# Starting a decoder-layer kernel with three matrix products of its cross-attention memory

## The chip, the cores and the metric

The kernel runs on one core of one Trainium2 chip. The time is device microseconds of one execution. Three runs of the kernel before took 683.46, 684.13 and 684.65 us (median 684.13). The profiled execution took 683.86 us, of which 682.0 us lie between its first and its last instruction.

## What is computed

One layer of a hybrid decoder over 256 tokens of width 1024, in float32. The normed input goes through one wide projection whose columns feed three branches: causal attention with 8 heads, a state-space scan with 4 groups, and cross-attention into 256 memory tokens with 4 heads. Gates merge the three, then come an output projection, a convolutional feed-forward network and a last norm. Cut to what the change touches:

```python
u = rms_norm(x, mix_norm_g)
proj = u @ w_in                      # q, k, v, z, xBC, dt, memory queries qm, three gates
kv = rms_norm(mem, mem_norm_g) @ w_mem_kv
km, vm = split(kv)                   # 4 heads of 256 columns each
s = (qm / 16) @ km.T                 # per head
o_mem = softmax(s) @ vm
merged = g0 * (o_attn @ w_br_attn) + g1 * (o_ssm @ w_br_ssm) + g2 * (o_mem @ w_br_mem)
h = x + merged @ w_out
out = rms_norm(h + conv_glu(rms_norm(h, ffn_norm_g)), final_norm_g)
```

A norm's factor is one number per memory token, so `rms_norm(mem) @ w` equals `factor * ((mem * mem_norm_g) @ w)`: the factor may be applied to the product.

## The kernel before, in words

**Chunks.** Every weight matrix passes through in chunks of 1 MB. Three slots (`w_raw`, 8 KB of each partition apiece) take them in turn, so a chunk is known by its round `r` and its slot `s`. For each chunk SyncE issues two DMAs (`load`, L292, or `load_wide`, L311) as soon as the slot's previous chunk has been split; ScalarE rounds it to `w_hi` (`split_hi`, L328) once TensorE is done with the slot's previous chunk; VectorE subtracts to get `w_lo` (`split_lo`, L334); and TensorE multiplies three times for each pair of operands, hi by hi, hi by lo and lo by hi (`three`, L362). A chunk of 256 columns is the moving or stationary side of 48 matmuls with 256 columns (`gemm_cols`, L339); a "wide" one, 512 rows by 512 columns, is the moving side of 24 matmuls with 512 columns (`wide_part`, L368).

**Order.** Nothing is scheduled by a compiler. Each engine's instructions stand in the order in which the source writes them, each engine runs its own queue strictly in that order, and semaphores hold it. So an instruction that waits holds up everything behind it on its engine.

**Start.** SyncE loads `x` first (L459, L460), then small tables and the first chunk of `w_in`. TensorE issues 13 matmuls on zeros meanwhile (`keep_warm`, L409, called at L585), then a small product for the attention bias, then turns `x` with 16 transposes (L600), after ScalarE's squares (L951), GpSimd's power (L1795) and VectorE's scaling (L1292). `tok_hi` (L963) and `tok_lo` (L1306) are split from the turned `x` column block by column block, and the first product, `first_part` (L604), follows.

**Stages.** Four groups of the scan (rounds 0 to 7), attention (`heads`, rounds RB = 8 to 11), memory and gate 1 (rounds RC = 12 to 15), the merge (rounds from RD = 16) and the rest. In the memory stage each of four rounds `i` does, on TensorE: a wide chunk of gate 1 (`gate1_part`, L748), the value product of the round before it with its probabilities (`mem_attend`, L774) and the turning of the next ones (`turn_mem_probs`, L766), a key chunk, a value chunk, and the scores of head `i` (`mem_scores`, L756). ScalarE and VectorE have a function `mem_head` (L1139, L1538) with the order of their side: queries, the split of the next chunks, keys, the state-space branch's normed output (`o_tmp`, `os_hi`, `os_lo`, L1564 to L1572), values, softmax. Gate 1's sum is taken out of PSUM banks 0 and 7 by VectorE (L1553) in rounds 1 and 3. The first product of the merge, `merge_part(0)` (L812), writes banks 0 and 1.

The normed memory itself is made during the attention stage: ScalarE squares `mem_nat`, the factor goes out to `m_factor_d` (L1107) and back as a row on all partitions (`m_factor`, L1115), and VectorE scales the transposed memory `mem_x` by the gain and the factor (`mem_scale`, L1455), which is split into `me_hi` and `me_lo`.

At the end of attention's last head ScalarE and TensorE leave turned probabilities in PSUM banks 3 and 4. ScalarE copies bank 3 (L1148), VectorE copies bank 4 (L1559) to `prob_t`; after that the banks may be written again, and TensorE's `attend(4)` may run.

## Time and profile before

| | us |
|---|---|
| median of three runs | 684.13 |
| the profiled execution | 683.86 |
| its span, first to last instruction | 682.0 |
| TensorE busy in the span | 674.6 |
| VectorE busy | 493.9 |
| ScalarE busy | 370.9 |
| first matmul on real weights starts | 9.86 |
| last matmul ends | 676.0 |

TensorE's busy time counts matmuls from issue to a modelled end, so neighbours overlap, and the matmuls on zeros count too: "99%" doesn't mean that all of it is work. What a group of matmuls takes is therefore read from the start of one group to the start of the next.

### The profile page before, as it was taken

How to read it: one execution, taken by the hardware profiler on the slowest of the kernel's cores; microseconds unless marked ns; L12 is line 12 of the kernel's file. 1: busy time of each engine (PE TensorE's matmuls, PEld its weight loads, DVE VectorE, ACT ScalarE, POOL GpSimd, SP SyncE). 2: the span in 40 equal slices, each digit the busy share in tenths (PEclk: the TensorE clock that was granted, in tenths of full speed). 3: DMA queues.
4: the chain of work that ended last, by engine and by line, in shares of the span. 5: the costliest groups of instructions: out<-in, count | busy, mean ns of one | idle time of the engine just before them, and what ended most of it. 6: DMA issues, size and time to landing. Idle time of an engine off the chain costs nothing.

```text
span 682.0 us, 11415 instructions
## 1 busy us (share of the span) xinstructions
PE 674.6 (99%) x4505; PEld 616.6 (90%) x4505; DVE 493.9 (72%) x619; ACT 370.9 (54%) x461; POOL 10.2 (2%) x21
## 2 busy tenths in 40 slices
PE   9999999999999999999999999999999999999996
PEld 6999999999999989999888888888899999999995
DVE  6886979696866766777755655556688777777796
ACT  6568767767555544555533333443555555555552
POOL 0000000000100000000000000000100000000001
PEclk9999999999999999999999999999999999999999
DMA  9775768569185456545566655565545555555521
GB/s 299 239 254 181 247 203 261 161 217 329 62 266 175 142 167 232 175 142 183 163 217 213 219 190 185 194 222 179 171 138 190 185 188 189 184 184 184 194 93 62
DMA packets 99743, 130.92 MB, mean 192 GB/s; under 512 B 5631, under 2 KB 73980, under 8 KB 99068
## 3 DMA queue, kind: packets, MB, share of 16 engines
q1 hardware_dynamic: 98164, 125.27, 56.0%
q10 hardware_dynamic: 1544, 5.16, 2.2%
q8 instruction: 25, 0.41, 0.3%
q14 instruction: 10, 0.08, 0.0%
HBM read 129.31 MB, written 2.68 MB: 194 GB/s over the span
## 4 chain that ended last, share of the span: by engine, by line
PE 98%; DVE 1%; issue 0%; POOL 0%; ACT 0%; POOLq 0%; DVEq 0%
PE ps L364 31%; PE ps L365 30%; PE ps L366 30%; PE ps L677 1%; PE ps L413 1%; PE ps L419 1%; PE ps L662 1%; PE ps L678 1%; PE ps L697 1%; PE ps L714 1%; PE ps L705 0%; DVE h_nat L1745 0%; PE ps L696 0%; PE ps L716 0%; PE ps L770 0%; PE ps L665 0%
## 5 line engine op out<-in xcount | busy, mean ns | idle before, releaser
L336 DVE TENSOR_TENSOR w_lo<-w_raw,w_hi 128x2048 fp32r<-128x2048 f32 x107 | 244.6, 2287 | 87.9 <-ACT w_hi L332 87.8
L332 ACT ACTIVATE w_hi<-w_raw 128x2048 fp32r<-128x2048 f32 x107 | 204.4, 1911 | 99.4 <-PE ps L366 93.9
L364 PE MATMUL ps<-tok_hi,w_hi 128*128 128x256 f32 x864 | 246.6, 285 | 0.4 <-DVE tok_lo L1306 0.4
L365 PE MATMUL ps<-tok_lo,w_hi 128*128 128x256 f32 x864 | 244.4, 283 | 0.0
L366 PE MATMUL ps<-tok_hi,w_lo 128*128 128x256 f32 x864 | 244.4, 283 | 0.0
L364 PEld LDWEIGHTS ps<-tok_hi,w_hi 128*128 128x128 f32 x864 | 165.7, 192 | 2.0 <-DVE w_lo L1300 0.8
L365 PEld LDWEIGHTS ps<-tok_lo,w_hi 128*128 128x128 f32 x864 | 165.7, 192 | 0.4
L366 PEld LDWEIGHTS ps<-tok_hi,w_lo 128*128 128x128 f32 x864 | 165.6, 192 | 0.0
L364 PE MATMUL ps<-w_hi,tok_hi 128*128 128x512 f32 x128 | 50.2, 392 | 0.0
L365 PE MATMUL ps<-w_lo,tok_hi 128*128 128x512 f32 x128 | 49.9, 390 | 0.0
L366 PE MATMUL ps<-w_hi,tok_lo 128*128 128x512 f32 x128 | 49.8, 389 | 0.0
L1242 ACT ACTIVATE conv_g<-pad_g,params 128x256 f32<-128x256 f32 x22 | 12.1, 595 | 38.5 <-DVE pad_g L1697 38.5
L1390 DVE SCALAR_TENSOR_TENSOR conv_a<-pad_x,params,conv_a 128x256 f32<-128x256 f32 x72 | 29.5, 479 | 0.3
L366 PEld LDWEIGHTS ps<-w_hi,tok_lo 128*128 128x128 f32 x128 | 24.0, 188 | 5.1
L364 PEld LDWEIGHTS ps<-w_hi,tok_hi 128*128 128x128 f32 x128 | 24.1, 188 | 4.9 <-issue 0.2
L365 PEld LDWEIGHTS ps<-w_lo,tok_hi 128*128 128x128 f32 x128 | 24.1, 188 | 4.8
L364 PE MATMUL ps<-w_hi,hid_hi 128*128 128x512 f32 x72 | 28.1, 391 | 0.0
L365 PE MATMUL ps<-w_lo,hid_hi 128*128 128x512 f32 x72 | 28.1, 391 | 0.0
L366 PE MATMUL ps<-w_hi,hid_lo 128*128 128x512 f32 x72 | 28.0, 389 | 0.0
L364 PE MATMUL ps<-w_hi,os_hi 128*128 128x512 f32 x64 | 25.1, 392 | 0.0
L365 PE MATMUL ps<-w_lo,os_hi 128*128 128x512 f32 x64 | 24.9, 390 | 0.0
L366 PE MATMUL ps<-w_hi,os_lo 128*128 128x512 f32 x64 | 24.9, 389 | 0.0
(268 smaller groups left out, 1003.3 us busy)
## 6 DMA issues: line engine op xcount, KB each, us to landing
w_raw<-w_in SPq DMA_DIRECT2D x94, 512.0 KB, 4.7
w_raw<-w_ffn_up SPq DMA_DIRECT2D x44, 512.0 KB, 4.3
w_raw<-w_ffn_down SPq DMA_DIRECT2D x22, 512.0 KB, 4.0
w_raw<-w_mem_kv SPq DMA_DIRECT2D x16, 512.0 KB, 4.4
w_raw<-w_br_ssm SPq DMA_DIRECT2D x16, 512.0 KB, 4.8
acs_b<-acs_d ACTq DMA_DIRECT2D x4, 1024.0 KB, 6.4
w_raw<-w_br_attn SPq DMA_DIRECT2D x8, 512.0 KB, 4.9
w_raw<-w_br_mem SPq DMA_DIRECT2D x8, 512.0 KB, 4.4
```

Source lines behind the costliest of these rows:

```text
L332: act.activation(w_hi[:, s, :], w_raw[:, s, :], ACT.Copy).then_inc(hi_ready[s], 1)
L336: dve.tensor_tensor(w_lo[:, s, :], w_raw[:, s, :], w_hi[:, s, :].bitcast(F32), ALU.subtract).then_inc(lo_ready[s], 1)
L364: pe.matmul(o, a[0], b[0], start=start, stop=False, **kw)
L365: pe.matmul(o, a[0], b[1], start=False, stop=False, **kw)
L366: return pe.matmul(o, a[1], b[0], start=False, stop=stop, **kw)
L413: pe.matmul(ps[:, 3, :].rearrange("p (a n) -> p a n", n=P), z, z.unsqueeze(1).to_broadcast([P, 4, P]), start=True, stop=True)
L419: return pe.transpose(ps[:, bank, o:o + P], src[:, t, k * P:(k + 1) * P], ident)
L662: mm = pe.transpose(ps[:, 3 + t, c * P:(c + 1) * P], conv_o[:, 2 + c, t * P:(t + 1) * P], ident)
L677: pe.matmul(o, x_dt[:, 0, h * SHD:(h + 1) * SHD], decay[:, h, 0:T], start=True, stop=False)
L678: mm = pe.matmul(o[:, P:T], x_dt[:, 1, h * SHD:(h + 1) * SHD], decay[:, h, T:T + P], start=False, stop=True)
L1242: act.activation(conv[:, j, :], pad[:, j, FTAPS - 1:], ACT.Identity, bias=cols_up[:, FTAPS, bass.ds(c, 1)], scale=cols_up[:, FTAPS - 1, ba ...
L1390: dve.scalar_tensor_tensor(conv_a[:, s, j, :], pad_x[:, s, j, tap:tap + T], cols_conv[:, tap, bass.ds(conv_tile(s, j, g), 1)], conv_a[:, s ...
```

## The change

The change computes three of the eight products of `w_mem_kv` first, while `x` is still on its way. Two value chunks (heads 0 and 1) and the key chunk of head 0 are multiplied with `mem_e`, the transposed memory with the gain but without the norm's factor; a small row `cols_mem` with the gain comes with `mix_cols`, on ScalarE's queue. The products are kept in `v_early` and `k_early`. The factor is applied at the beginning of the memory stage: VectorE makes `k_scaled`, ScalarE and VectorE multiply by `m_cols`, the factor as a column, while they split. That column is a third small DMA on ScalarE's queue. `x` is loaded behind the memory and its weights; 8 instead of 13 matmuls on zeros stand ahead. All rounds of the scan and of attention have numbers one higher. The memory stage has three rounds of chunks instead of four, in the order of `MEM`, and the last value product but one, `mem_attend(3)`, moves ahead of the merge. The number of matmuls is the same but for the 5 on zeros.

```diff
-X_HALVES = ((4, 0), (5, 0), (6, 0), (7, 0), (1, 0), (2, 0), (3, 0), (4, T))
+X_HALVES = ((4, 0), (6, 0), (7, 0), (3, 0), (2, 0), (2, T), (5, 0), (5, T))
-RA, RB, RC, RD, RE, RF, RG = 0, 8, 12, 16, 20, 24, 26
+RA, RB, RC, RD, RE, RF, RG = 1, 9, 13, 16, 20, 24, 26
+MEM = (("gate", 0), ("key", 1), ("gate", 1), ("key", 2), ("value", 0), ("gate", 2), ("key", 3), ("value", 1), ("gate", 3))
...
             x_tiles = x[0].rearrange("(t p) d -> p t d", p=P)
+            for n, ks in enumerate((slice(0, 1), slice(1, 2), slice(2, HK))):
+                sp.dma_start(mem_e[:, ks, :], mem_tiles[:, ks, :]).then_inc(first_in[n], 16)
+                sp.dma_start(slot[0][:, ks, :], w_v[:, ks, :]).then_inc(first_in[n], 16)
+            sp.dma_start(mem_e[:, HK:, :], mem_tiles[:, HK:, :]).then_inc(second_in[0], 16)
+            for n in range(2):
+                ks = slice(2 * n, 2 * n + 2)
+                sp.dma_start(slot[1][:, ks, :], w_v[:, HK + 2 * n:HK + 2 * n + 2, :]).then_inc(second_in[n], 16)
+            load(sp, 0, 2, w_mem_kv[0], 0)
             sp.dma_start(x_nat[:, 0, 0:D], x_tiles[:, 0, :]).then_inc(x_in[0], 16)
             sp.dma_start(x_nat[:, 1, 0:D], x_tiles[:, 1, :]).then_inc(x_in[1], 16)
...
-            for i in range(4):
-                load_wide(sp, RC + i, 0, wi, (GATEC + D + RW * (i // 2), i % 2))
-                load(sp, RC + i, 1, w_mem_kv[0], CW * i)
-                load_wide(sp, RC + i, 2, w_mem_kv[0], (D + RW * (i // 2), i % 2))
-                if i in (1, 2):
+            for n, (kind, i) in enumerate(MEM):
+                r, s = RC + n // SLOTS, n % SLOTS
...
+                if n in (3, 6):
+                    i = n // SLOTS
                     sp.wait_ge(qm_low, i)
...
-            keep_warm(pe, 13)
+            keep_warm(pe, 8)
...
+            for s in range(2):
+                for k in range(HK):
+                    pe.wait_ge(m_lo, HK * s + k + 1)
...
+                    for t in range(NT):
+                        cut, at = slice(t * P, (t + 1) * P), HK * s + k
+                        mm = three(pe, ps[:, V_BANKS[t], :], (mem_e_hi[:, at, cut], mem_e_lo[:, at, cut]),
+                                   (rows_of(w_hi, s, k), rows_of(w_lo, s, k)), at == 0, at == KT - 1)
+                mm.then_inc(gemm_done[s], 1)
...
             pe.wait_ge(oa_lo_s, 2)
-            gate1_part(0)
+            pe.wait_ge(bank_free[0], RC + 1)
+            mem_chunk(0)
             attend(3)
             turn_probs(4)
-
-            gemm_cols(pe, RC, 1, me_hi, me_lo, tiles=(m_lo, 1))
+            pe.wait_ge(m_lo, 2 * KT)
+            mem_chunk(1)
+            pe.wait_ge(pt_ready, 8)
+            mem_scores(0)
+            mem_chunk(2)
+            attend(4)
+            turn_mem_probs(1)
+            mem_chunk(3)
+            mem_scores(1)
             pe.wait_ge(oa_lo_s, 3)
-            gemm_wide(pe, RC, 0, me_hi, me_lo)
-            mem_scores(0)
-            for i in range(1, 4):
-                gate1_part(i)
-                if i == 1:
-                    attend(4)
-                else:
-                    mem_attend(i - 1)
-                turn_mem_probs(i)
-                gemm_cols(pe, RC + i, 1, me_hi, me_lo)
-                gemm_wide(pe, RC + i, i % 2, me_hi, me_lo)
-                mem_scores(i)
+            mem_chunk(4)
+            mem_attend(1)
+            turn_mem_probs(2)
+            pe.wait_ge(bank_free[0], RC + 2)
+            pe.wait_ge(bank_free[2], RC + 2)
+            mem_chunk(5)
+            mem_scores(2)
+            mem_chunk(6)
+            mem_attend(2)
+            turn_mem_probs(3)
+            mem_chunk(7)
+            mem_scores(3)
+            mem_chunk(8)
+            mem_attend(3)
+            turn_mem_probs(4)
...
             pe.wait_ge(bank_free[0], RD + 1)
-            pe.wait_ge(bank_free[1], RD + 1)
+            pe.wait_ge(bank_free[2], RD + 1)
             pe.wait_ge(os_lo_s, 1)
             merge_part(0)
-            mem_attend(3)
-            turn_mem_probs(4)
```

On ScalarE and VectorE the calls of `mem_head` become lists that are written out. Two places of the order are shown.

VectorE at the beginning of the memory stage, before: behind the split of the stage's third chunk come the queries, the split of the next chunk, the last attention output and the copy of bank 4 (`prob_t`).

```order
L336 TENSOR_TENSOR w_lo<-w_raw,w_hi 128x2048 [waits hi_ready2]
L1541 TENSOR_TENSOR qm_lo<-qm,qm_hi 128x512 [waits qm_hi_s]
L336 TENSOR_TENSOR w_lo<-w_raw,w_hi 128x2048 [waits hi_ready0]
L1472 TENSOR_TENSOR oa_lo<-ps,oa_hi 128x512 [waits oa_hi_s]
L1559 COPY prob_t<-ps 128x384 [waits p_turned]
```

The same place now:

```order
L345 TENSOR_TENSOR w_lo<-w_raw,w_hi 128x2048 [waits hi_ready2]
L1670 TENSOR_TENSOR k_scaled<-k_early,m_factor 128x512
L1635 TENSOR_TENSOR qm_lo<-qm,qm_hi 128x512 [waits qm_hi_s]
L1619 TENSOR_TENSOR km_lo<-k_scaled,km_hi 128x512 [waits km_hi_s]
L1676 SCALAR_TENSOR_TENSOR vm_lo_136<-v_early,m_cols,vm_hi 128x512 [waits vm_hi_s]
L1676 SCALAR_TENSOR_TENSOR vm_lo_137<-v_early,m_cols,vm_hi 128x512 [waits vm_hi_s]
L345 TENSOR_TENSOR w_lo<-w_raw,w_hi 128x2048 [waits hi_ready0]
L1562 TENSOR_TENSOR oa_lo<-ps,oa_hi 128x512 [waits oa_hi_s]
L1681 COPY prob_t<-ps 128x384 [waits p_turned]
```

Four instructions for the early products stand ahead of the split, and the copy of bank 4 stands behind all of it; on ScalarE the rounding of the key and of the two value tiles stands ahead of `next_hi(0)` in the same way.

VectorE in round 3 of the memory stage, before: gate 1's second eviction (L1553, which frees banks 0 and 7) stands early in the round.

```order
L1541 TENSOR_TENSOR qm_lo<-qm,qm_hi 128x512 [waits qm_hi_s]
L1535 TENSOR_TENSOR om<-ps,om 128x2x256 [waits om_hi_s]
L1529 TENSOR_TENSOR mprob_lo<-ps,mprob_hi 128x512 [waits mpt_hi_s]
L1553 TENSOR_TENSOR g_78<-ps,bias_g_75 128x512 [waits bias_g1_in,gemm_done0]
L1553 TENSOR_TENSOR g_78<-ps,bias_g_75 128x512
L336 TENSOR_TENSOR w_lo<-w_raw,w_hi 128x2048 [waits hi_ready0]
L1529 TENSOR_TENSOR km_lo<-ps,km_hi 128x512 [waits km_hi_s]
L336 TENSOR_TENSOR w_lo<-w_raw,w_hi 128x2048 [waits hi_ready1]
```

VectorE at the end of the memory stage, now, from the split that follows value chunk 1 to gate 1's second eviction (L1642):

```order
L345 TENSOR_TENSOR w_lo<-w_raw,w_hi 128x2048 [waits hi_ready1]
L1714 TENSOR_TENSOR vm_lo_136<-ps,vm_hi 128x512 [waits vm_hi_s]
L1714 TENSOR_TENSOR vm_lo_137<-ps,vm_hi 128x512 [waits vm_hi_s]
L1658 TENSOR_REDUCE msoft<-ps 128x2 [waits ms_mm]
L1660 TENSOR_SCALAR msoft<-msoft 128x2 [waits ms_max]
L1664 RECIPROCAL msoft<-msoft 128x2 [waits mp_exp]
L1667 TENSOR_SCALAR mprob<-mprob,msoft 128x256 [waits mp_rec]
L1667 TENSOR_SCALAR mprob<-mprob,msoft 128x256
L1647 SCALAR_TENSOR_TENSOR o_tmp<-v_ssm,params,rstd_g 128x256 x4
L1653 TENSOR_TENSOR os_lo<-o_tmp,os_hi 128x1024 [waits os_hi_s]
L1642 TENSOR_TENSOR g_78<-ps,bias_g_75 128x512 [waits bias_g1_in,gemm_done2]
L1642 TENSOR_TENSOR g_78<-ps,bias_g_75 128x512
```

The second eviction stood ahead of that round's key, value and softmax; now it stands behind the last head's softmax and the last piece of the branch output.

On TensorE two short products, `mem_attend(3)` and `turn_mem_probs(4)`, now stand between gate chunk 3 and the merge; before, a key product, a value product and the scores stood there. TensorE's wait on `bank_free[2]` ahead of `merge_part(0)` is for both tiles of gate 1's second eviction.

## Rows read from the trace of the kernel before

**Rows 1.** The page, part 1: busy time of each engine.

```profile
PE 674.6 (99%) x4505; PEld 616.6 (90%) x4505; DVE 493.9 (72%) x619; ACT 370.9 (54%) x461; POOL 10.2 (2%) x21
```

**Rows 2.** Waits of TensorE over the whole span: the one on real work.

```profile
PE ps L364 <- DVE tok_lo L1306: 0.4, 1, 0.4
```

**Rows 3.** Timeline of the first 12 us: start, duration, engine, line.

```profile
0.98 5.73 PE L413 MATMUL ps<-zero_s 128*128 128x512 bf16 x13 [0.98 <-DVE zero_s L1283]
4.16 1.06 ACT L951 ACTIVATE junk_x<-x_nat 128x1025 f32<-128x1025 f32 x1 [1.92 <-DMA x_nat<-x]
6.76 0.63 ACT L957 ACTIVATE w_hi<-w_raw 128x512 fp32r<-128x512 f32 x1 [0.21 <-DMA w_raw<-w_in]
7.34 1.84 PE L600 MATMUL ps<-square_c,x_nat 128*128 128x128 f32 x14
9.86 0.35 PE L364 MATMUL ps<-tok_hi,w_hi 128*128 128x256 f32 x1 [0.45 <-DVE tok_lo L1306]
10.42 0.36 PE L364 MATMUL ps<-tok_hi,w_hi 128*128 128x256 f32 x1
```

**Rows 4.** DMA view of the first 18 us in 40 equal slices.

```profile
GB/s 0 0 0 55 191 373 337 428 419 364 242 312 327 324 323 269 316 311 295 230 264 302 360 353 357 360 346 342 334 366 373 344 369 350 360 369 362 348 355 346
```

**Rows 5.** Windows, TensorE: key chunk, scores, gate chunk, value product, turning.

```profile
256.28:262.02 5.74, 5.74 (x51) 1.00 0.69 248
267.59:269.02 1.43, 1.43 (x13) 1.00 0.63 190
269.02:274.49 5.47, 5.47 (x26) 1.00 0.42 145
294.36:295.79 1.43, 1.43 (x14) 1.00 0.00 0
295.79:296.14 0.35, 0.35 (x6) 1.00 0.00 0
```

**Rows 6.** Timeline of VectorE at the beginning of the memory stage.

```profile
254.40 2.28 DVE L336 TENSOR_TENSOR w_lo<-w_raw,w_hi 128x2048 fp32r<-128x2048 f32 x1
256.60 0.68 DVE L1541 TENSOR_TENSOR qm_lo<-qm,qm_hi 128x512 fp32r<-128x512 f32 x1
261.14 0.68 DVE L1472 TENSOR_TENSOR oa_lo<-ps,oa_hi 128x512 fp32r<-128x512 f32 x1
261.74 0.55 DVE L1559 COPY prob_t<-ps 128x384 f32<-128x384 f32 x1
```

**Rows 7.** Timeline of ScalarE in the memory stage.

```profile
262.32 0.60 ACT L1161 ACTIVATE km_hi<-ps 128x512 fp32r<-128x512 f32 x1 [3.42 <-PE ps L366]
262.81 1.91 ACT L332 ACTIVATE w_hi<-w_raw 128x2048 fp32r<-128x2048 f32 x1
289.50 1.07 ACT L1172 ACTIVATE vm_hi<-ps 128x512 fp32r<-128x512 f32 x2
```

**Rows 8.** Timeline of VectorE in rounds 1 and 3 of the memory stage.

```profile
286.83 1.67 DVE L1565 SCALAR_TENSOR_TENSOR o_tmp<-v_ssm,params,rstd_g 128x256 f32<-128x256 f32 x4
290.77 1.28 DVE L1576 TENSOR_TENSOR vm_lo<-ps,vm_hi 128x512 fp32r<-128x512 f32 x2
291.97 0.68 DVE L1579 TENSOR_REDUCE msoft<-ps 128x2 f32<-128x512 f32 x1
294.14 0.62 DVE L1586 TENSOR_SCALAR mprob<-mprob,msoft 128x256 f32<-128x256 f32 x2
318.55 1.28 DVE L1553 TENSOR_TENSOR g<-ps,bias_g 128x512 f32<-128x512 f32 x2
```

**Rows 9.** Timeline of SyncE's DMA issues in the memory stage.

```profile
257.63 1.80 SPq L530 DMA_DIRECT2D bias_g<-b_gate  x1
277.93 0.47 SPq L530 DMA_DIRECT2D bias_g<-b_gate  x1
```

**Rows 10.** Windows behind the last matmul: TensorE's busy time is the second number, PEclk stands behind the engines.

```profile
676.00:679.00 3.00, 0.01 (x1) 0.00 (x0) 2.00 (x6) 2.31 (x7) 1.37 (x3) 1.00 0.33 122
679.00:682.00 3.00, 0.00 (x0) 0.00 (x0) 0.13 (x1) 0.00 (x0) 0.00 (x0) 0.56 0.63 227
```

More of the change, by code:

```diff
@@ L592, in _ @@
+            pe.wait_ge(first_lo, 7)
+            open_bank(pe, 1)
+            for j in range(2):
+                for half in range(2):
+                    if half and not j:
+                        pe.wait_ge(lo_ready[2], 2)
+                    mm = cols_part(pe, 2, j, range(HK * half, HK * half + HK), ps[:, 1, j * T:(j + 1) * T], mem_e_hi,
+                                   mem_e_lo, start=False, stop=False, skip_group_check=True)
+            mm.then_inc(gemm_done[2], 1)
             pe.wait_ge(const_in, 16)
-            pe.wait_ge(x_in[0], 16)
@@ L1587, in mem_head @@
                                       ALU.mult).then_inc(mp_norm, 1)
-                split_lo(dve, r + 1, 2)
-            mem_head(0, first=True)
-            for i in range(1, 4):
-                mem_head(i)
+            dve.tensor_tensor(k_scaled[:], k_early[:], m_factor[:].unsqueeze(1).to_broadcast([P, 2, T]),
+                              ALU.mult).then_inc(m_scaled, 1)
+            queries_lo(0)
+            low(None, km_hi, km_lo, km_hi_s, 1, m_lo, k_scaled[:])
+            for t in range(NT):
+                dve.wait_ge(vm_hi_s, t + 1)
+                dve.scalar_tensor_tensor(vm_lo[t][:], v_early[:, t, :], m_cols[:, t:t + 1], vm_hi[:, t, :].bitcast(F32),
+                                         ALU.mult, ALU.subtract).then_inc(m_lo, 1)
@@ new lines, in _ @@
+            mem_attended_lo(2)
+            low(4, mprob_hi, mprob_lo, mpt_hi_s, 3, mpt_ready)
+            next_lo(7)
+            for t in range(NT):
+                dve.wait_ge(vm_hi_s, NT + t + 1)
+                dve.tensor_tensor(vm_lo[t][:], ps[:, V_BANKS[t], :], vm_hi[:, t, :].bitcast(F32),
+                                  ALU.subtract).then_inc(bank_free[1], 1)
+            mem_max(3)
+            mem_norm(3)
+            branch_lo(3)
+            gate1_out(1)
+            next_lo(8)
@@ L1595, in merge_split_lo @@
+            mem_attended_lo(3)
+            low(4, mprob_hi, mprob_lo, mpt_hi_s, 4, mpt_ready)
             def merge_split_lo(n):
```

451 lines of the change are left out of this document (258 added, 193 removed).

## The prediction

> **What bounds the kernel now.** I read the page's busy times first: TensorE is busy for 674.6 of 682.0 us, VectorE and ScalarE for 493.9 and 370.9 [rows 1]. Then TensorE's waits: on real work there is one, 0.4 us long [rows 2]. So from 9.86 us to the end TensorE never stands still, and only two things can change the time: what TensorE does or loses before 9.86 us, and new waits later. The timeline of the first 12 us shows the first of these [rows 3]: zeros until 6.7 us, 14 of the 16 transposes from 7.34, the first matmul on weights at 9.86, and an unbroken stream from 10.42. Then I read the memory stage, where the change rewrites the order: how long TensorE's pieces take [rows 5], and the chains on VectorE and ScalarE between them [rows 6 to 8]. There the reader is to see that nobody waits now only because a key chunk and a value chunk lie between each result and its use.
>
> **The start.** The change removes no matmul but 5 on zeros; three chunks of about 5.5 us each move from the memory stage to the front. So the gain is what TensorE loses at the start.
>
> Before: at 10.42 us TensorE has done 16 transposes (14 take 1.84, so 2.1) and three matmuls (0.4). The other 7.9 us are lost [rows 3].
>
> Now: the first product needs a piece of the memory and of the value weights, 384 KB. The DMA slices (0.45 us each) add up to 430 KB at 3.15 us, so to 393,000 bytes at 3.0 [rows 4]; the 512 KB of the first tile of x are through at 3.4 by the same sum, and ScalarE read them from 4.16 [rows 3], 0.8 later. So ScalarE starts at 3.8. It takes 0.63 for the weights [rows 3], VectorE 0.68 and then a quarter of 1.67 for the memory piece [rows 6, 8], and with some 0.2 for the hand-overs the first matmul starts at 5.8. The 8 zero matmuls last until 0.98 + 8 x 0.44 = 4.5, and the bias product, whose table now goes first on ScalarE's own queue, lies behind them. Gain: 7.9 - 5.8 = 2.1 us. Bounds of the start: 5.3 (hand-overs overlap better) and 6.8 (the gain row, for which ScalarE waits first, lands a microsecond late).
>
> Will the stream hold? A chunk of 1 MB takes 3 us at some 350 GB/s [rows 4] and 5.5 to 5.7 on TensorE [rows 5]. The memory, three chunks, x and the first chunk of `w_in` are 6 MB and land at about 20.5; TensorE reaches the transposes at 5.8 + 2 x 5.47 + 5.74 = 22.5, so x is scaled in time. VectorE makes one `tok_lo` in 0.42 against 0.36 for TensorE's three matmuls, but it starts during the transposes. I cost this at 0; without that cover it would be 8 x 0.06 = 0.5. The later rounds keep their order and distances, with x 12 us later for everyone.
>
> The clock: 13 zero matmuls of 512 columns take 5.73 us, 0.44 each, the pace of the lower level, 1.2 GHz, to 6.7 us [rows 3]; a gate chunk's 24 take 5.47, 0.23 each, the pace of 2.4 GHz [rows 5]. (The clock column reads full in both; there is no record ahead of the first change.) Now real matmuls start at 5.8, with a short idle gap ahead of them. If the clock rises where it did, about 1.2 us run at half pace: 0.6 lost. If it rises only as long after 5.8 as it did after 0.98, 5.7 us do: 2.9 lost. I take 0.6, since zeros and bias fill most of the time ahead. The Trainium skill (TensorE: Matmul & The Clock Gate, Part 1) says that the array starts throttled and that sustained activity releases it; the trace agrees, with 0.44 against 0.23 us. By that rule, taken strictly, the gap would start the wait anew and the start would lose 0.8 us instead of gaining 1.5.
>
> So the start is worth 2.1 - 0.6 = **1.5 us**; bounds -0.8 and +2.6.
>
> **The memory stage, first wait.** `mem_scores(0)` writes banks 3 and 4, so it waits for VectorE's copy of bank 4. Before, a value chunk stood between key chunk and scores; now the scores follow key chunk 1 at once. I put the new order on the times of before. TensorE ends key chunk 1 where key chunk 0 ended, at 262.02 [rows 5]. VectorE's split of the third chunk starts at 254.40, the next instruction at 256.60 [rows 6]. That is now `k_scaled`, to 257.28. ScalarE waits for it, then rounds the key and two value tiles at 0.53 apiece (two take 1.07) and only then splits, 1.91 [rows 7]: 257.31 + 1.59 + 1.91 = 260.81. VectorE's split takes 2.20 to its successor, the attention output 0.60, the copy 0.55 [rows 6]: 260.84 + 3.35 = 264.19, and TensorE starts at 264.3. Wait: **2.3 us**. Queued behind the scores is the rest of the stage. Bounds: 1.5 (a `k_scaled` that overlaps better) and 3.0.
>
> **The memory stage, second wait.** `merge_part(0)` needs banks 0 and 7, that is gate 1's second eviction. Before, VectorE did it at 318.55 [rows 8], some 9 us ahead of the merge; so it cost nothing, and its cover was a key chunk, a value chunk and the scores. Now gate chunk 3 is the last of the stage, and the eviction stands behind a chain that begins when value chunk 1 ends. From that end on:
>
> - ScalarE starts after 0.30 (its read of the key after 262.02) and splits in 1.91 [rows 7];
> - VectorE splits in 2.20 to its successor [rows 6] and takes out the value's low part, 1.20 from 290.77 to 291.97 [rows 8];
> - softmax of head 3, with ScalarE's exponent inside: 2.79, from 291.97 to 294.76;
> - `o_tmp` to the end of `os_lo`, with ScalarE's `os_hi` inside: 3.94, from 286.83 to the successor at 290.77;
> - the eviction, 1.28 [rows 8], and 0.2 to TensorE.
>
> Sum: 13.8 us. TensorE meanwhile has the scores, gate chunk 3, `mem_attend(3)` and a turning: 1.43 + 5.47 + 1.43 + 0.35 = 8.7 [rows 5]. Wait: **5.1 us**, some of it already at `mem_scores(3)`, whose keys stand behind a like chain one chunk earlier. VectorE runs this chain without a gap, so an earlier start of one link doesn't shorten it. Bounds: 3.5 (links overlap more) and 5.8.
>
> A smaller term: SyncE now waits for the first query's low part (257.9) and issues the bias row ahead of value chunk 0's weights; that issue took 1.80 and 0.47 us [rows 9], so they are issued at 258.4 to 259.7 and land some 5 us later. ScalarE wants them at 262. Up to 2.7 us late on ScalarE and VectorE, but TensorE's next need, the turned probabilities, has about 3 us in hand. I cost it at 0, bound +1.5. The DMA of the factor column, `k_early`'s copy and the two `v_early` copies lie beside products of 5.5 us: 0. The three chunks that are gone from the stage take 6.6 us of VectorE's splits with them, but those filled gaps.
>
> **The sum.** 683.86 - 1.5 + 2.3 + 5.1 = 689.8 us. The median of the three runs lies 0.3 above the profiled execution, the end effects are rounded, and I predict **689.7**.
>
> **The rivals.** *The stage keeps its cover* (ends faster): VectorE has three splits less and TensorE finds every operand ready, because ScalarE and VectorE run ahead. Place: the scores of head 0 and the first product of the merge. It decides where the chain behind value chunk 1 is 8.7 us or shorter, and the copy of bank 4 ends before 262. For it: VectorE is free for 28% of the span [rows 1]. Against: the chain is 13.8 us of dependent rows, not of load. Time: 683.9 - 1.5 = 682.4, with the best start 681.3.
>
> *One wait decides*: the second is mostly covered, the first stands, or the other way round. 683.9 - 1.5 + 2.3 = 684.7, up to 687.4 with 5.1 and not 2.3. For it: each stands on a place of its own. Against: the same row durations make both.
>
> *The clock falls in the second wait.* The last matmul ends at 676.0; until 679.0 the clock column reads 1.00, and 0.56 in the last 3 us [rows 10]: about 3.3 us after TensorE went idle it went to the lower level. A wait of 4 to 5 us at the merge may do the same; the way back, by the start, costs 3 to 6 us at half pace, 1.5 to 3 us. Time: 691.3 to 692.8. For it, row 10; against it, part of the 5.1 us falls at `mem_scores(3)`, so the longest gap may be only 4. The same page of the Trainium skill says that an idle stretch throttles the array again; rows 10 agree, with 0.56.
>
> *The early start doesn't happen*: the first pieces land late or the clock stays low; the start is worth 0 and the stage costs 7.4: 691.3.
>
> **How the numbers follow.** Both waits, 0.58; the clock falls as well, 0.12; the early start fails beside them, 0.12; one wait, 0.10; cover kept, 0.08. A measurement of this kernel can tell 0.2%, 1.4 us, from no change: 682.8 to 685.5. Faster: the kept cover and a little of the single wait, 0.09. Same: half of the single wait, 0.06. Slower: 0.85. The range leaves out the kept cover and some of the clock's case: from 685.5 (a single wait) to 693.0 (both waits, late weights, or the clock falls).
>
> **What would show it.** In the changed profile the first product starts at 5.8 us and there is no wait until the memory stage. TensorE's waits show about 2.3 us ahead of the scores of head 0, ended by VectorE's copy of bank 4, and 4 to 5 us ahead of the first product with the branch output, ended by VectorE's g, with up to 1 us at the scores of head 3. The prediction is wrong if these waits are absent or under 1 us, if TensorE waits for a DMA at the start, or if its matmuls run at half pace for long behind 5.8 us.

## The result and the profile after

The changed kernel took 697.52 us (median of six runs, 696.62 to 698.62), the kernel before 683.87 beside it (683.46 to 684.65). The ratio is 1.0201, 95% interval 1.0191 to 1.0211: slower by 13.7 us. Forecast were 689.7 and a range up to 693.0, so the direction was right and the size was not. The profiled execution of the changed kernel took 698.53 us with a span of 696.4, 14.4 above the span before.

The page, part 1, and TensorE's waits over the whole span (total, times, longest), of the changed kernel, beside [rows 1, 2]:

```profile
PE 679.5 (98%) x4500; PEld 619.9 (89%) x4500; DVE 498.8 (72%) x632; ACT 375.5 (54%) x475; POOL 10.6 (2%) x21
```

```profile
PE ps L373 <- issue: 3.4, 1, 3.4
PE ps L373 <- DVE prob_t L1681: 2.1, 1, 2.1
PE ps L373 <- DVE mem_e_lo L1385: 2.1, 1, 2.1
PE ps L373 <- DVE km_lo L1619: 1.5, 1, 1.5
...
PE ps L808 <- DVE mprob L1667: 0.8, 2, 0.6
```

Where one wait of 0.4 us stood there are now six of 9.9 us in all. In order of time: 2.1 at the first product of the start; 2.1 at the scores of head 0; 0.8 at two turnings of probabilities; 1.5 at the scores of head 3; and 3.4 ahead of the merge, which the profile puts down to "issue". TensorE's busy time has grown as well, by 4.9 us with five matmuls fewer. No work was added: matmuls at half pace make up 5.6 us (2.9 at the start and 2.7 at the merge, worked out below), and the five zeros that are gone some 2 us the other way. The rest wasn't traced.

The start, on the timeline of the changed kernel (beside [rows 3]): the first weights on ScalarE, the first product, and two products from 13 us on.

```profile
5.79 0.63 ACT L1005 ACTIVATE w_hi<-w_raw 128x512 fp32r<-128x512 f32 x1 [2.44 <-DMA w_raw<-w_mem_kv]
7.60 0.79 PE L373 MATMUL ps<-w_hi,mem_e_hi 128*128 128x512 f32 x1 [2.06 <-DVE mem_e_lo L1385]
12.88 0.63 PE L373 MATMUL ps<-w_hi,mem_e_hi 128*128 128x512 f32 x1
13.85 0.40 PE L373 MATMUL ps<-w_hi,mem_e_hi 128*128 128x512 f32 x1
27.34 1.91 PE L647 MATMUL ps<-square_c,x_nat 128*128 128x128 f32 x16
```

The last row is the turning of `x`, which follows the moved work. The first weights come 2 us later than worked out, the first product 1.8 later, and from 7.60 to 13.44 us the products follow each other at 0.43 us instead of 0.23. The DMA view of the first 18 us (40 slices of 0.45, beside [rows 4]) shows why ScalarE waited:

```profile
GB/s 0 0 0 18 163 226 213 205 100 96 223 341 296 328 362 398 373 369 341 346 405 389 419 398 405 394 371 364 353 353 353 341 380 389 389 378 432 431 338 339
```

From 1.8 to 5 us it moves 96 to 226 GB/s, where x moved 337 to 428 from 2.25 to 4.5 us before.

The end of the stage, on VectorE's timeline and in windows around the merge (the second number is TensorE's busy time, PEclk stands behind the engines):

```profile
333.28 1.28 DVE L1714 TENSOR_TENSOR vm_lo<-ps,vm_hi 128x512 fp32r<-128x512 f32 x2
...
337.18 1.67 DVE L1647 SCALAR_TENSOR_TENSOR o_tmp<-v_ssm,params,rstd_g 128x256 f32<-128x256 f32 x4
339.97 1.22 DVE L1653 TENSOR_TENSOR os_lo<-o_tmp,os_hi 128x1024 fp32r<-128x1024 f32 x1 [1.12 <-ACT os_hi L1212]
341.11 1.28 DVE L1642 TENSOR_TENSOR g<-ps,bias_g 128x512 f32<-128x512 f32 x2
```

```profile
338.00:341.00 3.00, 1.12 (x10) 0.88 (x8) 1.88 (x4) 2.12 (x2) 0.00 (x0) 1.00 0.00 0
341.00:348.00 7.00, 5.50 (x13) 4.38 (x14) 4.79 (x6) 2.77 (x4) 0.00 (x0) 0.51 0.62 169
348.00:356.00 8.00, 8.00 (x36) 6.61 (x36) 2.29 (x1) 1.92 (x1) 0.00 (x0) 1.00 1.02 370
```

```profile
342.50 0.77 PE L373 MATMUL ps<-w_hi,os_hi 128*128 128x512 f32 x1 [3.38 <-issue]
```

TensorE is done with the turning at 339.1. The eviction of gate 1 (L1642) ends at 342.4, behind the whole chain of the branch output, and the merge starts at 342.50, in the last row; so "issue" is this wait. Meanwhile the granted clock fell to the lower level, 0.51 of full, until 348.

### The profile page after: what moved, and what is told of

It is laid out like the page before. It is cut to its first block, busy times and chain, and to the rows that moved or that the text cites. A ratio compares the mean times of both kernels' runs of the same rounds, so it can differ in the third digit from the quotient of the medians.

```text
span 696.4 us, 11454 instructions
## 1 busy us (share of the span) xinstructions
PE 679.5 (98%) x4500; PEld 619.9 (89%) x4500; DVE 498.8 (72%) x632; ACT 375.5 (54%) x475; POOL 10.6 (2%) x21
## 4 chain that ended last, share of the span: by engine, by line
PE 88%; DVE 6%; ACT 2%; DMA 2%; issue 1%; SPq 0%; POOL 0%; POOLq 0%; DVEq 0%; ACTq 0%
PE ps L373 28%; PE ps L374 27%; PE ps L375 27%; DVE w_lo L345 2%; DMA w_raw<-w_mem_kv 2%; PE ps L707 1%; ACT w_hi L341 1%; DVE o_tmp L1647 1%; PE ps L708 1%; PE ps L428 1%; PE ps L692 1%; PE ps L727 1%; DVE qm_lo L1635 0%; ACT mprob L1221 0%; DVE h_nat L1873 0%
## 5 line engine op out<-in xcount | busy, mean ns | idle before, releaser
L345 DVE TENSOR_TENSOR w_lo<-w_raw,w_hi 128x2048 fp32r<-128x2048 f32 x105 | 240.2, 2287 | 91.7 <-ACT w_hi L341 91.7
L341 ACT ACTIVATE w_hi<-w_raw 128x2048 fp32r<-128x2048 f32 x105 | 200.5, 1911 | 110.4 <-PE ps L375 93.2
```

Of the source, the lines that this page charges most:

```text
L341: act.activation(w_hi[:, s, :], w_raw[:, s, :], ACT.Copy).then_inc(hi_ready[s], 1)
L345: dve.tensor_tensor(w_lo[:, s, :], w_raw[:, s, :], w_hi[:, s, :].bitcast(F32), ALU.subtract).then_inc(lo_ready[s], 1)
```

## The experiments

Fourteen kernels, each with the kernel before beside it on the same chip (683.47 to 683.59). Unless it is said otherwise, each is the changed kernel with one edit.

**1. The eviction ahead of the branch output.**

```diff
             mem_norm(3)
+            gate1_out(1)
             branch_lo(3)
-            gate1_out(1)
             next_lo(8)
```

> VectorE takes gate 1's second sum out of PSUM right after head 3's softmax instead of behind the branch output (o_tmp, os_lo); nothing else moves. Theory (the eviction's place makes the wait, and the wait makes the clock fall): the eviction ends at about 338.6 us instead of 342.4, the first product of the merge follows the turning at 339.0, the clock stays at 1.00, and of 697.5 us some 3.5 of the wait and 2.7 of the clock go: 691.3. Rival one (the chain behind it is as late: branch output or next split holds the second or third merge product): half comes back, 694. Rival two (the clock's fall at 341 has another cause than the wait): only 3.5 go, 694.0, and the clock column still shows 0.5 there.

Measured: 691.96 us (691.09 to 693.01). The wait ahead of the merge is gone, and so is the fall of the clock. The window of this kernel at the merge:

```profile
341.00:348.00 7.00, 7.00 (x32) 5.82 (x31) 4.72 (x4) 4.39 (x5) 0.00 (x0) 1.00 0.92 308
```

32 matmuls where there were 13. Exchanging two calls on an engine that is busy for 72% gave back 5.6 us: this wait came from the place of the eviction in VectorE's order.

**2. Zeros in the wait.** The wait stays, TensorE is kept at work:

```diff
+            keep_warm(pe, 14)
             pe.wait_ge(bank_free[0], RD + 1)
```

> 14 matmuls on zeros (0.23 us each at the full clock, 3.2 us) stand behind the last turning, in the wait ahead of the merge; the wait itself stays. Theory (TensorE's idle time makes the clock fall, and the fall costs 2.7 us by itself): the first merge product still starts at 342.5 us, the clock stays at 1.00, 694.8. Rival (the pace behind 341 us is slow for another reason, such as operands that come late): no change, 697.5.

Measured: 695.45 us (694.77 to 695.95), 2.1 less. In the same window the clock is 1.00 and 30 matmuls run:

```profile
341.00:348.00 7.00, 6.64 (x30) 5.41 (x30) 3.81 (x4) 2.03 (x3) 0.00 (x0) 1.00 0.63 212
```

So of the 5.6 us of run 1 some 2 were the clock and 3.5 the wait. The split isn't sharp: in this execution the clock fell at another wait instead, at 282.2 us, by the scores of head 0, so the theory's 2.7 are not fully seen; and it rose early at the start, at 5.72 instead of 13.44 us, which is worth 1.4 us there (last section).

**3. The copies first.** `attended_hi(3)`, `attended_lo(3)` and the two copies to `prob_t` stand behind the queries, ahead of keys, values and the split.

```diff
             queries_lo(0)
+            attended_lo(3)
+            dve.wait_ge(p_turned, 8)
+            dve.tensor_copy(prob_t[:, 1, :], ps[:, 4, 0:3 * P]).then_inc(pt_ready, 1)
...
             next_lo(0)
-            attended_lo(3)
-            dve.wait_ge(p_turned, 8)
-            dve.tensor_copy(prob_t[:, 1, :], ps[:, 4, 0:3 * P]).then_inc(pt_ready, 1)
             next_lo(1)
```

> On ScalarE and VectorE the third attention output and the copies of the turned probabilities go ahead of the rounding of the early key and values, instead of behind those and the split of the third chunk. Theory (the copy of bank 4 is late only by its place in the queue): the 2.3 us ahead of the scores of head 0 go, 695.2, and the waits at the end of the stage stay. Rival (the moved 1.2 us push keys, values and splits, and the wait comes back at the scores of head 1 or key chunk 2, or at the end of the stage): 696.5 or more.

Measured: 698.18 us (697.33 to 699.24), no gain. The wait at the scores is gone, and a longer one stands at the turned probabilities. TensorE's waits, then ScalarE, VectorE and SyncE on this kernel's timeline:

```profile
PE ps L808 <- DVE mprob L1667: 3.3, 1, 3.3
```

```profile
276.41 0.35 SPq L556 DMA_DIRECT2D bias_g<-b_gate  x1
276.80 0.94 SPq L327 DMA_DIRECT2D w_raw<-w_mem_kv  x2
285.25 1.92 ACT L341 ACTIVATE w_hi<-w_raw 128x2048 fp32r<-128x2048 f32 x1 [5.78 <-DMA w_raw<-w_mem_kv]
287.20 2.29 DVE L345 TENSOR_TENSOR w_lo<-w_raw,w_hi 128x2048 fp32r<-128x2048 f32 x1 [5.40 <-ACT w_hi L341]
289.41 0.68 DVE L1658 TENSOR_REDUCE msoft<-ps 128x2 f32<-128x512 f32 x1
```

ScalarE stands 5.8 us for the weights of value chunk 0, and VectorE behind it; the maximum for the softmax of head 0 is queued behind that split. SyncE issued the weights at 276.8 only, because the bias row ahead of them waits for the queries' low part. Run 5 moves that row. This is the place that the prediction named and costed at 0.

**4. Zeros at the start.** Four more zeros behind the bias product.

```diff
             mm.then_inc(bias_mm, 1)
+            keep_warm(pe, 4)
```

> Four more matmuls on zeros (0.44 us each, 1.8 us) behind the bias product, so that TensorE's 2.06 us of idle time ahead of the first product shrink to 0.3; the product starts at 7.6 us as before. Theory (the gap delays the rise of the clock from about 7 us to 13.4 and costs 2.9 us): the clock is up at 7 to 8 us and the time is 694.6. Rival (the rise depends on real products or on something else): the clock still rises at 13.4, 697.5.

Measured: 696.81 us (694.83 to 697.55). This doesn't decide: in the profiled execution the clock was up at 4.25 already, so the four zeros took half as long and 1.36 us of the gap stayed.

**5. The bias row behind the weights**, with run 3's edit:

```diff
-                if n in (3, 6):
+                if n in (5, 8):
```

> As the run with the copies first, and SyncE issues the two bias rows of gate 1, with their waits for the queries' low part, two chunks later, behind the loads that stood behind them. Theory (value chunk 0's weights arrive at 285 us because SyncE stands at the wait for the queries until 276.4, and this second limit gave back what the copies gained): the weights are there when ScalarE asks at 279.5, both waits (2.1 at the scores of head 0, 3.3 at the turned probabilities) go, and 0.2 at the next turning: 694.5, where the copies alone left 698.2. Rival (the chain of ScalarE and VectorE for the softmax of head 0 is itself too long): a wait of over 1 us stays at the turned probabilities, 696 or more.

Measured: 692.53 us (691.66 to 694.44): 5.6 below run 3, 5.0 below the changed kernel, and TensorE waits at the start, at the scores of head 3 and at the merge only. The theory expected 694.5. The 2 us more lie within what the clock does by chance at the start and at the merge (below); how much is the start's and how much the merge's wasn't told apart.

**6. The stage reordered**: runs 1 and 5 together, the keys of head 3 ahead of a split on both engines, and the maximum of head 3 ahead of a split.

```diff
+            keys_hi(3)
             next_hi(6)
-            keys_hi(3)
...
+            mem_max(3)
             next_lo(7)
```

> The run above, and gate 1's second eviction ahead of the branch output (worth 5.6 us by itself), and the keys of head 3 rounded ahead of the split that stood before them (1.5 us at the scores of head 3), and head 3's maximum ahead of a split. Theory (five late operands make all of the stage's loss): 697.5 - 2.1 - 0.9 - 1.5 - 5.6 = 687.4, no wait of TensorE over 0.3 us behind the start; what is left over the kernel before, some 3.5 us, is the start. Rival (VectorE and ScalarE have too much to do between, and a new wait opens): 689 or more, with a wait over 1 us in the stage.

Measured: 685.80 us (685.07 to 686.61), ratio to the kernel before 1.0031 (1.0018 to 1.0043). All of TensorE's waits of this kernel:

```profile
PE ps L373 <- DVE mem_e_lo L1385: 2.7, 1, 2.7
PE ps L422 <- DVE zero_s L1373: 1.0, 1, 1.0
```

None is left behind the start. The scores of attention's head 0 and the last matmul, in the changed kernel and in this one:

```profile
266.78 0.38 PE L726 MATMUL ps<-k_t,q_t 128*128 128x128 f32 x2
690.12 0.28 PE L375 MATMUL ps<-w_hi,end_lo 128*128 128x256 f32 x1
```

```profile
265.32 0.38 PE L726 MATMUL ps<-k_t,q_t 128*128 128x128 f32 x2
676.82 0.28 PE L375 MATMUL ps<-w_hi,end_lo 128*128 128x256 f32 x1
```

Between the two rows TensorE takes 423.3 us in the changed kernel and 411.5 here, 11.8 less. The kernel before takes 428.1 (247.60 to 675.73), which is 411.5 and the 16.7 of moved work, within 0.1. So the whole loss of the memory stage, 11.8 us, were operands that stood at the wrong place of a queue, and no lack of capacity: the same instructions do the same work. The five moves weren't all tried one by one, so the share of the maximum alone and of the keys alone isn't known. The theory's sum was 687.4; the 1.6 us more are again of the size of the clock's chance at the start. What is left, 2.2 us in the medians, is the start.

**7, 8, 14. Why the first weights are late.** In run 7 the two tables go first on SyncE's queue; in run 8 three pieces of the memory go on ScalarE's queue and the weights are issued from 0.73 us on; in run 14 the whole memory goes ahead of the weights.

```diff
# run 7
-            act.dma_start(cols_both[:], mix_cols).then_inc(gain_in, 16)
-            act.dma_start(bias_s[0:BUCKETS + 1, :], bias_cols).then_inc(relb_in, 16)
+            sp.dma_start(cols_both[:], mix_cols).then_inc(gain_in, 16)
+            sp.dma_start(bias_s[0:BUCKETS + 1, :], bias_cols).then_inc(relb_in, 16)
# run 8
-                sp.dma_start(mem_e[:, ks, :], mem_tiles[:, ks, :]).then_inc(first_in[n], 16)
+            act.dma_start(mem_e[:, 0:1, :], mem_tiles[:, 0:1, :]).then_inc(first_in[0], 16)
             act.dma_start(cols_both[:], mix_cols).then_inc(gain_in, 16)
             act.dma_start(bias_s[0:BUCKETS + 1, :], bias_cols).then_inc(relb_in, 16)
+            act.dma_start(mem_e[:, 1:2, :], mem_tiles[:, 1:2, :]).then_inc(first_in[1], 16)
+            act.dma_start(mem_e[:, 2:HK, :], mem_tiles[:, 2:HK, :]).then_inc(first_in[2], 16)
# run 14
                 sp.dma_start(mem_e[:, ks, :], mem_tiles[:, ks, :]).then_inc(first_in[n], 16)
+            sp.dma_start(mem_e[:, HK:, :], mem_tiles[:, HK:, :]).then_inc(second_in[0], 16)
+            for n, ks in enumerate((slice(0, 1), slice(1, 2), slice(2, HK))):
                 sp.dma_start(slot[0][:, ks, :], w_v[:, ks, :]).then_inc(first_in[n], 16)
-            sp.dma_start(mem_e[:, HK:, :], mem_tiles[:, HK:, :]).then_inc(second_in[0], 16)
```

> The two small tables (gains and bias) go first on SyncE's queue, ahead of the memory and weights, instead of on ScalarE's own queue. Theory one (the small packets of ScalarE's queue slow the first pieces down at 2 to 4 us): the slow stretch goes, ScalarE starts on the first weights at 4.7 us (3.8 as predicted and two issues of 0.45), against 5.3 to 5.8 now, and the first product comes at 6.5. Theory two (the first packets of the weights are slow of themselves): the slow stretch moves with them, ScalarE starts at 6.3 to 6.7, the first product comes at 8.3 and the time is up by 0.5 to 1.

> Three of the memory's pieces go on ScalarE's queue, so SyncE issues the first weights at 0.73 instead of 1.17 us, and the second and third at 1.2 and 1.6. Theory one (issuing one after the other is what makes the first pieces late): ScalarE starts on the first weights at about 5.0, as soon as its own table load is over, and on the second piece at once behind it; first product at 6.8. Theory two (the first packets of the weights are slow of themselves, whatever their queue): ScalarE starts no earlier than 5.3, and the products no earlier than 7.1.

> The changed kernel with all 1 MB of the memory ahead of the first weights on SyncE's queue. Theory (the weights' first packets, rows of 2 KB that lie 8 KB apart, are slow of themselves): between 2 and 4 us the DMAs move 250 GB/s and more, as they did with x before, and the slow stretch (150 to 200 GB/s, packets of 1 us) comes behind it, with the first 2 KB packets. Rival (whatever comes first is slow): 150 to 200 GB/s from 2 to 4 us on the memory's own 1 KB packets, and none behind.

Measured: 697.00 and 697.68 (two executions each) and 700.64 us (one); ScalarE starts on the first weights at 6.17, 6.03 and 10.08. In run 8 it was the gain row, behind a piece of memory on ScalarE's queue, that ScalarE waited for at 6.03, so that row doesn't decide; the DMA's own view does. GB/s in the first 10 us (40 slices of 0.25) of runs 7, 8 and 14:

```profile
GB/s 1 0 0 0 0 0 2 29 102 75 54 166 332 168 238 49 135 156 156 197 266 283 348 320 275 320 307 320 266 274 311 279 307 242 197 238 279 295 320 324
```

```profile
GB/s 0 0 0 0 0 0 0 66 131 229 152 127 180 217 234 329 323 322 347 342 361 370 360 336 315 336 336 348 393 389 361 373 369 369 393 377 393 381 369 385
```

```profile
GB/s 0 0 0 0 0 0 12 172 200 226 190 333 291 336 381 283 156 90 127 324 299 328 307 201 123 135 147 209 246 287 303 332 315 328 295 303 352 311 295 311
```

With the tables out of the way the slow stretch is still there (3.3 to 5 us, 49 to 238), so ScalarE's queue isn't the cause. With the weights first it begins with them, from 1.8 to 3.8 us (66 to 234). With the memory first the memory runs at 283 to 381 from 2.8 to 4, and a slow stretch follows at 5.8 to 7 us (123 to 209), with the first 2 KB packets, those of the weights. So the weights' first packets are slow wherever they stand. The rival isn't excluded for the memory: in run 14 its own first microsecond, 1.75 to 2.75 us, is slow as well (172 to 226, where the theory had 250 and more), and there is another dip at 4 to 4.8 us (90 to 156) on the memory alone, which no theory here explains. Run 7's first product came at 7.97, towards theory two's 8.3, but the time isn't up by the 0.5 to 1 that this theory had.

**9 to 11. The zeros.** Run 9 is run 6 with 13 zeros, run 11 the kernel before with 8. Run 10 is run 9 with a shorter chain to the first product: each piece of memory is rounded ahead of its weights, with semaphores of its own.

```diff
# run 9 (run 11: the same line of the kernel before, the other way round)
-            keep_warm(pe, 8)
+            keep_warm(pe, 13)
# run 10, ScalarE (VectorE alike: mem_first_lo ahead of first_lo_part)
-                act.wait_ge(first_in[min(k, 2)], 32)
+                act.wait_ge(mem_in[min(k, 2)], 16)
+                mem_first_hi(k)
+                act.wait_ge(piece_in[k], 16)
                 act.activation(rows_of(w_hi, 0, k), rows_of(w_raw, 0, k), ACT.Copy).then_inc(
                     first_hi if k < HK - 1 else hi_ready[0], 1)
-                mem_first_hi(k)
```

> The run with the reordered stage (685.8), and 13 matmuls on zeros at the start again, as before the change, instead of 8. Theory (the idle 2 to 2.7 us ahead of the first product make the clock fall, or rise late): at the lower level the zeros last until 6.7 us and the bias product until 7.4, TensorE is idle for under 0.5 us, the clock is up at 7 us or earlier and doesn't fall again; the fall from 7.1 to 10.5 us that the run without them showed cost 1.7, so 684.1 to 684.5. Rival (where the clock rises at 4 us by itself, the five zeros take half as long and the gap stays): 685.3 to 685.8, with a fall in the record between 6 and 13 us.

> The run above with 13 zeros, and a shorter chain to the first product: each piece of memory is rounded and subtracted ahead of its weights (it lands earlier), every piece has its own semaphore, and the third and fourth weight rows are loaded apart. Theory (the chain behind the landing, 0.63 + 0.49 + 0.69 + 0.48 us and the hand-overs, is part of what makes the start late): two of the four links leave the chain and the first product comes 0.9 us earlier, at 6.5 to 6.8 us; against the run above 0.5 to 0.9 less, 683.4 to 684.0. Rival (the weights' pieces arrive too slowly for TensorE at the full clock, so an earlier first product only waits for the second to fourth piece): no gain over the run above, and TensorE waits of 0.4 us and more between 8 and 12 us.

> The kernel before with 8 instead of 13 matmuls on zeros, nothing else. The first transposes still come at 7.34 us, so TensorE is idle for some 1.9 us from 5.5 on. Theory (fewer zeros by themselves cost the clock at the start): the clock rises later or falls once behind 7 us, 3.4 to 6.5 us at half pace, 685.1 to 686.5. Rival (the zeros' number doesn't matter, since the change's loss at the start is all in the late first product): 683.4 to 683.7.

Measured: 685.20 (684.69 to 685.99), 684.99 (684.50 to 685.70) and 684.34 us (683.63 to 685.41; ratio 1.0011, 1.0001 to 1.0021). In run 9 the gap stays at 1.4 us, as its rival said, though the clock didn't fall in the profiled execution; the median is 0.6 lower, and the intervals of the two ratios overlap. At the full clock TensorE then waits again, for the third piece:

```profile
11.72 0.50 PE L373 MATMUL ps<-w_hi,mem_e_hi 128*128 128x512 f32 x1 [1.14 <-DVE mem_e_lo L1385]
```

Run 10's first product didn't come earlier but at 8.71: the copy of the bias row stands ahead of the pieces on VectorE and waits for the bias product, which the 13 zeros hold back:

```profile
7.28 0.29 DVE L1387 COPY bias_row<-ps 72x128 f32<-72x128 f32 x1 [5.63 <-PE ps L619]
```

In run 11 both sides miss. The clock is up at 9.92 us in the profiled execution instead of 6.91, and the transposes run at half pace. TensorE in run 11:

```profile
6.90 3.18 PE L600 MATMUL ps<-square_c,x_nat 128*128 128x128 f32 x14
...
10.16 0.36 PE L364 MATMUL ps<-tok_hi,w_hi 128*128 128x256 f32 x1
```

The transposes take 3.18 us instead of 1.84, but the first product comes only 0.3 later: there the low clock lies beside a chain on other engines. In the changed kernel it lies on the products themselves. The median of run 11 is 0.8 up; where the other 0.5 us go wasn't traced.

**12, 13. First product or arrival.** Run 12 is run 10 with the bias copy behind the pieces and 11 zeros; run 13 also loads the second half of the memory in two DMAs, each ahead of its own weights.

```diff
# run 12, VectorE: behind the pieces, ahead of the scaling of x
-            dve.wait_ge(bias_mm, 1)
-            dve.tensor_copy(bias_row[0:2 * Q + HEADS, :], ps[0:2 * Q + HEADS, 0, 0:P]).then_inc(bias_copied, 1)
...
+            dve.wait_ge(bias_mm, 1)
+            dve.tensor_copy(bias_row[0:2 * Q + HEADS, :], ps[0:2 * Q + HEADS, 0, 0:P]).then_inc(bias_copied, 1)
# run 13, SyncE
-            sp.dma_start(mem_e[:, HK:, :], mem_tiles[:, HK:, :]).then_inc(mem_in[3], 16)
             for n in range(2):
+                ks = slice(HK + 2 * n, HK + 2 * n + 2)
+                sp.dma_start(mem_e[:, ks, :], mem_tiles[:, ks, :]).then_inc(mem_in[3 + n], 16)
                 ks = slice(2 * n, 2 * n + 2)
```

> The run with stage and start reordered (684.99), where the copy of the bias row stood on VectorE ahead of the first pieces and held the first product until 8.7; here the copy stands behind all pieces, and 11 zeros instead of 13 stand ahead. Theory (arrival of the weights bounds the stream, not its first product): the first product comes at 7.0 to 7.3, but TensorE then waits for the second and for the fifth piece (the fifth is rounded from 12.7 and ready at 14.0, where the stream of the run before reached it at 14.2), so only 0.2 to 0.3 is gained: 684.7. Rival (the late first product is what costs): 1.4 to 1.6 are gained, 683.5, no slower than the kernel before.

> As the run with the copy behind, and the second half of the memory is loaded as two DMAs of 256 KB, each right ahead of the two weight rows that it goes with, so that the fifth weight row stands 256 KB earlier in the queue. Theory (arrival bounds the stream): 256 KB at some 370 GB/s are 0.7 us, the fifth piece is ready at 13.3 instead of 14.0, and the time falls by up to 0.7 against the run with the copy behind: 684.0 to 684.3, at most level with the kernel before (683.56). Rival (first product decides, or the later pieces arrive no earlier): no change, 684.7.

Measured: 684.62 (684.51 to 686.19) and 684.23 us (683.83 to 685.00). The first product comes at 7.16 in run 12, 1.5 earlier than in run 10, and 0.4 is gained, near the 0.2 to 0.3 of the theory and far from the 1.4 to 1.6 of the rival. The waits that the theory expected aren't there in the profiled execution, though: its clock fell from 7.2 to 10.6 us, the products ran at half pace, and the turning of `x` begins where it did in run 10. Runs 10, 12 and 13:

```profile
25.68 1.91 PE L651 MATMUL ps<-square_c,x_nat 128*128 128x128 f32 x16
```

```profile
25.71 1.91 PE L651 MATMUL ps<-square_c,x_nat 128*128 128x128 f32 x16
```

```profile
24.79 1.91 PE L652 MATMUL ps<-square_c,x_nat 128*128 128x128 f32 x16
```

So this run alone doesn't tell the arrival of the pieces from the clock; that arrival binds at the full clock is seen in run 9's wait above. With the arrivals in order another 0.4 goes, as the theory said, but the clock of run 13's profiled execution also rose at 4.73 and didn't fall, so the gain isn't shown to be the pieces' alone. Run 13 stands at 1.0010 of the kernel before (1.0000 to 1.0019): level within what a measurement can tell, 13.3 us below the changed kernel. No version was found that beats the kernel before.

## Why the prediction was wrong

**First wait, predicted 2.3 us: right.** Key chunk 1 ends, 2.1 us pass, and VectorE's copy of bank 4 ends the wait. On the timeline of the changed kernel the chain is the one that was put together from [rows 6, 7]:

```profile
280.18 2.29 DVE L345 TENSOR_TENSOR w_lo<-w_raw,w_hi 128x2048 fp32r<-128x2048 f32 x1 [1.00 <-ACT w_hi L341]
282.39 0.68 DVE L1562 TENSOR_TENSOR oa_lo<-ps,oa_hi 128x512 fp32r<-128x512 f32 x1
282.99 0.55 DVE L1681 COPY prob_t<-ps 128x384 f32<-128x384 f32 x1
```

```profile
281.18 0.28 PE L375 MATMUL ps<-me_hi,w_lo 128*128 128x256 f32 x1
...
283.60 0.39 PE L373 MATMUL ps<-km_hi,qm_hi 128*128 128x256 f32 x1 [2.14 <-DVE prob_t L1681]
```

**Second wait, predicted 5.1 us in two places: right.** 3.4 at the merge and 1.5 at the scores of head 3 are 4.9; the division was a little off, with 4 to 5 expected at the merge and up to 1 at the scores. Run 1 shows the cause and the place of the first; run 6, which moves the keys of head 3 among other things, leaves no wait at the second. "VectorE runs this chain without a gap" isn't so to the letter: it stands 1.1 us for ScalarE's `os_hi` (L1653 above), which the sum had inside its link. That an earlier start of one link doesn't shorten the chain was tried by no run; the eviction didn't belong into the chain, and run 1 took it out.

**The clock in the second wait: the rival was taken for the unlikely case.** The argument was that a gap of 4 us or less might not bring the clock down. A wait of 3.4 us did. It stayed down from 341.1 to 348.0 in the profiled execution, and half of 5.5 us of work, 2.7, was lost; run 2 measured 2.1 in the median of four executions. The Trainium skill (TensorE: Matmul & The Clock Gate, Part 1) says that an idle stretch throttles the array; this trace agrees, with 0.51.

**Late weights of value chunk 0, costed at 0, bound 1.5: wrong.** The 0.8 at the turned probabilities is theirs, inside the bound. ScalarE was to stand up to 2.7 us for them and stood 4.6, since it could start on them only 8 us after their issue at 277.48 and not 5:

```profile
285.59 1.92 ACT L341 ACTIVATE w_hi<-w_raw 128x2048 fp32r<-128x2048 f32 x1 [4.58 <-DMA w_raw<-w_mem_kv]
```

The delay was seen, and set against the "about 3 us in hand" of TensorE. Run 3 shows the full price once the first wait no longer hides it: ScalarE stands 5.8 us there and TensorE waits 3.3, so what was in hand was about right and the delay was priced too low. The two limits stood one behind the other: taking the first away gave nothing (run 3), taking both away gave 5.0 (run 5), of which 3 were expected and 2 are of the size of the clock's chance. The second was not taken away alone.

**The start, predicted a gain of 1.5, bounds -0.8 to 2.6: the step that failed.** The prediction's sum puts the transposes at 22.5 us, 23.1 with the clock. The start is worth nothing where they begin at 24.6 (the 7.9 us lost before and 16.7 of moved work). They began at 27.34, 4.2 late. Two terms make 4.1 of it:

- *The first product at 5.8: it came at 7.60, 1.8 late.* The sum over the DMA slices took the rate of x's loads for the weights; runs 7, 8 and 14 show that these start at 50 to 240 GB/s.
- *The clock, 0.6: the products ran at half pace from 7.60 to 13.44, 2.9 lost.* The text had this case as its strict reading, 2.9 lost, and chose the milder one.

The second term hides a third, which the prediction put at 0: it checked whether the stream holds by whole chunks at 350 GB/s, and not by the pieces of the first one. In run 5 the clock is up from 5.53 us on and the first product comes at 7.33, so the turning of `x` could begin at 24.0; it begins at 25.44. Most of these 1.4 us are lost in the first two chunks, where TensorE waits for later pieces. Its waits for pieces (total, times, longest; the longest is that for the first product) and that row:

```profile
PE ps L373 <- DVE mem_e_lo L1385: 2.2, 2, 1.8
```

```profile
25.44 1.91 PE L647 MATMUL ps<-square_c,x_nat 128*128 128x128 f32 x16
```

So of the way from 22.5 to 27.34 some 2.9 us are the late arrival of the weights, and a clock that is up in time gives back 1.4 (run 2) to 1.9 (run 5) and not 2.9.

From the heads' scores the loss is 2.5 us: TensorE reaches those of head 0 at 247.60 before and at 266.78 after (the latter row stands under run 6), 19.2 later, and 16.7 of it is moved work.

```profile
247.60 0.38 PE L696 MATMUL ps<-k_t,q_t 128*128 128x128 f32 x2
```

Put together: 689.7, and 4.0 for the start (1.5 gain, 2.5 loss), 2.7 for the clock at the merge and 0.8 for the late weights make 697.2, and the two waits came out 0.4 shorter than forecast. The median is 697.5, but these terms are read from the profiled execution, which took 698.5, so between 1 and 2 us of it aren't in the sum. Part of them is that a wait costs more than its listed time: from the last matmul ahead of the first wait to the next one it is 2.42 us (281.18 to 283.60), where the pace is 0.12, so 2.3 and not 2.1.

## What to carry to other kernels

When work is taken out of a stage, look for every result that used to be ready because that work stood between it and its use, and move the short instruction that makes it (an eviction, a copy, a subtraction) ahead of long ones on its engine; here four such moves and one DMA gave back 11.7 of 13.7 us in the medians without a change of work. Expect a second limit right behind the first. Before work is moved to the front, price its first transfers, piece by piece, by rows of the same tensor and shape, and ask what a low clock would lie on: the products themselves took 0.43 us each instead of 0.23, while transposes beside other engines' chains made the first product only 0.3 us later (run 11).

## What the runs showed of the hardware

**The clock's rise isn't tied to the program.** Six executions with the same instructions up to the memory stage (first products at 7.1 to 7.6 us; rise, fall and second rise from the trace's record of the granted clock):

| | clock rises | falls again | transposes begin |
|---|---|---|---|
| changed kernel | 13.44 | no | 27.34 |
| run 1 | 13.35 | no | 27.17 |
| run 3 | 4.91 | 8.32 to 11.74 | 26.64 |
| run 2 | 5.72 | no | 25.97 |
| run 6 | 3.72 | 7.13 to 10.54 | 25.87 |
| run 5 | 5.53 | no | 25.44 |

The window of run 6 over its fall shows 7 matmuls in 3.4 us at 0.50, and 17 in as much behind it:

```profile
7.13:10.54 3.41, 3.12 (x7) 2.48 (x8) 2.01 (x5) 2.38 (x5) 0.00 (x0) 0.50 1.02 355
10.54:14.00 3.46, 3.46 (x17) 2.82 (x15) 2.68 (x7) 2.55 (x7) 0.00 (x0) 1.00 1.07 374
```

The same start, with its idle stretch of some 2 us, so varies by 2 us from execution to execution (25.44 to 27.34), and the fall at the merge lasted 6.8 us in one execution and 3.4 in others (runs 3 and 5). This fits the six times of the changed kernel, three near 696.6 and three near 698.5, but only one of them was profiled, so it isn't shown. The same page of the Trainium skill says that the gate's timing isn't set by the kernel's start and that, in sustained activity, the point of change varies by half a microsecond; the first part agrees with the table. The variation here, from 3.72 to 13.44, is almost 10 us, with an idle stretch in the activity, so it isn't the page's case. A wait of 2.1 to 2.2 us, at the scores of head 0, was followed by a fall of the clock in runs 2, 8 and 14 and not in the changed kernel and runs 1, 4 and 7.

**The first packets of a tensor can be slow** (`w_mem_kv` in runs 7, 8 and 14): some 1.3 to 2 us at 50 to 240 GB/s, where in run 8 the DMAs move 315 to 393 from 3.75 us on. Why, no run here tells.
